# First stage of a two-layer GLA / NSA decoder step: ScalarE's first copy, ScalarE's order, products of zeros ahead of the turning

## What is computed

```python
def rms_norm(x, g):
    y = x * lax.rsqrt(jnp.mean(x * x, axis=-1, keepdims=True) + EPS)
    return y * g
...
hp = rms_norm(xp, norm_mix[i])
hs = rms_norm(xs, norm_mix[i])
...
z = h @ w_in
q, k, v, r, gr = jnp.split(z, ...)
log_alpha = jax.nn.log_sigmoid(gr @ w_gate2 + b_gate) / GLA_TAU
```

## Time and profile before

| | us |
|---|---|
| median of 3 runs | 1865.19 |
| lowest and highest run | 1858.73, 1870.34 |
| the profiled execution | 1865.75 |
| its span, first to last instruction | 1863.9 |
| PE busy in the span | 1728.0 |
| VectorE, ScalarE, GpSimd busy | 985.2, 724.1, 445.4 |

### The profile page before, as it was taken

How to read it: one execution, slowest core, us unless ns; L and a number is a source line. 1 busy time by engine, 2 the same in 40 slices (tenths; PEclk the granted TensorE clock), 3 DMA queues, 4 the chain that set the end, 5 groups by cost and what they waited for, 6 DMA issues and landing times.

```text
span 1863.9 us, 33488 instructions
## 1 busy us (share of the span) xinstructions
PE 1728.0 (93%) x13943; PEld 1602.3 (86%) x13951; DVE 985.2 (53%) x1518; ACT 724.1 (39%) x1227; POOL 445.4 (24%) x378
## 2 busy tenths in 40 slices
PE   7999989999999998999898897898889999999996
PEld 6989767999999997999787796676757999999996
DVE  5070457644444455466777865778524644444443
ACT  4352343332323232332455644677652332323230
POOL 4354234000000002444222122687803000000000
PEclk9999879999999999999899898899998999999998
DMA  4212123222222222331322110002373322222211
GB/s 173 91 46 91 49 97 111 118 91 91 91 90 90 90 90 98 109 119 46 114 103 84 53 58 1 1 2 91 136 316 137 136 91 91 91 90 90 90 45 46
DMA packets 25617, 170.13 MB, mean 91 GB/s; under 512 B 2146, under 2 KB 13970, under 8 KB 15706
## 3 DMA queue, kind: packets, MB, share of 16 engines
q1 hardware_dynamic: 22346, 131.18, 18.8%
q0 software_dynamic: 3152, 37.26, 5.3%
HBM read 156.26 MB, written 12.17 MB: 90 GB/s over the span
## 4 chain that ended last, share of the span: by engine, by line
PE 75%; DVE 12%; ACT 7%; issue 3%; POOL 2%; DMA 1%; ACTq 0%; SPq 0%; DVEq 0%; PEldq 0%; POOLq 0%
PE slot L2241 55%; PE slot L2497 3%; PE slot L2210 2%; ACT phase L1486 2%; PE slot L2505 2%; PE slot L2324 2%; POOL phase L1003 1%; PE slot L2475 1%; DVE xt_rest L1967 1%; PE slot L2285 1%; PE slot L2635 1%; PE slot L2695 1%; DVE base L1581 1%; DVE phase L1682 1%; PE slot L2579 1%
## 5 line engine op out<-in xcount | busy, mean ns | idle before, releaser
L1285 ACT ACTIVATE w_high<-weights 128x1024 fp32r<-128x1024 f32 x128 | 135.3, 1060 | 258.4 <-PE slot L2241 250.0
L2241 PE MATMUL slot<-h_high,w_high 128*128 128x260 f32 x1024 | 208.0, 284 | 0.0
L2241 PE MATMUL slot<-h_high,w_rest 128*128 128x260 f32 x1024 | 207.5, 284 | 0.0
L2241 PE MATMUL slot<-h_rest,w_high 128*128 128x260 f32 x1024 | 207.4, 284 | 0.0
L2241 PE MATMUL slot<-u_high,w_high 128*128 128x260 f32 x1024 | 206.3, 283 | 0.0
L2241 PE MATMUL slot<-u_rest,w_high 128*128 128x260 f32 x1024 | 206.0, 283 | 0.0
L2241 PE MATMUL slot<-u_high,w_rest 128*128 128x260 f32 x1024 | 206.0, 283 | 0.0
L1818 DVE TENSOR_TENSOR w_rest<-weights,w_high 128x1024 fp32r<-128x1024 f32 x128 | 156.0, 1222 | 31.5 <-ACT w_high L1285 31.5
L2241 PEld LDWEIGHTS slot<-h_high,w_high 128*128 128x128 f32 x1024 | 159.2, 190 | 0.2
L2241 PEld LDWEIGHTS slot<-h_high,w_rest 128*128 128x128 f32 x1024 | 159.0, 190 | 0.0
L2241 PEld LDWEIGHTS slot<-h_rest,w_high 128*128 128x128 f32 x1024 | 158.8, 190 | 0.0
(11 more groups left out here) (419 smaller groups left out, 4132.5 us busy)
## 6 DMA issues: line engine op xcount, KB each, us to landing
weights<-in_wt SPq DMA_DIRECT2D x47, 2048.0 KB, 7.8
weights<-in_state SPq DMA_DIRECT2D x2, 2048.0 KB, 8.8
out<-weights SPq DMA_DIRECT2D x2, 2048.0 KB, 8.3
weights<-in_w SPq DMA_DIRECT2D x2, 2048.0 KB, 9.0
out<-phase SPq DMA_DIRECT2D x6, 512.0 KB
x_rows<-residual SPq DMA_DIRECT2D x1, 2080.0 KB, 6.8
residual<-x_rows SPq DMA_DIRECT2D x1, 2080.0 KB, 11.0
phase<-in_x_prompt SPq DMA_DIRECT2D x2, 1024.0 KB, 6.5
```

The source lines that it names most:

```text
L1285: nc.scalar.activation(w_part[k % 4][0][:, :, :], ring[:, s, :, 128 * (k % 4):128 * (k % 4) + 128], ACT.Copy).then_inc(w_high_ready, 1)
L2241: last = mm(ps[0:w.shape[2], a, 0:HT], w[:, k, :], m[:, k, HT * a:HT * a + HT], start=k == 0 and w is high and m is x_high, stop=k == DC - ...
```

## The change

Four things change, all in the first stage.

- ScalarE begins with a copy of one column (`eps_col` to a column of `rstd_col`, which is written anew later). It waits only for `bf_ready`, and the table load goes with it.
- The high part of `wgr` is made after chunk 2 and no longer after chunk 4. It takes the place of a square, so the squares follow one chunk later from there on.
- The high part of the first weight piece is made after the square that follows chunk 6, ahead of chunk 7, and no longer behind chunk 7 and the square of chunk 6. The squares of the last three chunks then come in a row.
- PE makes nine products of zeros ahead of the first turning, into slot 0. They wait for `bf_ready`. The function that makes them is moved up in the code.

```diff
             act.wait_ge(bf_ready, 5)
+            link(nc.scalar.activation(rstd_col[:, 0:1], eps_col, ACT.Copy))
             act.wait_ge(ident_in, 48)
             for c in range(DC):
                 act.wait_ge(x_ready, c + 1)
                 nc.scalar.activation(gh_part[0][:, c, :], xT[:, c, :], ACT.Copy, scale=P("norm")[:, c:c + 1])\
                     .then_inc(mixed_high_ready, 1)
-                if c:
-                    square_of_input(c - 1)
-                if c == 4:
+                if c == 2:
                     act.wait_ge(gla_small_in, 48)
                     nc.scalar.activation(wgr_part[0][:, :, :], wgr, ACT.Copy).then_inc(wgr_high_ready, 1)
-            gla_weights_high(0)
+                elif c:
+                    square_of_input(c - 1 - (c > 2))
+                if c == 6:
+                    gla_weights_high(0)
+            square_of_input(DC - 2)
             square_of_input(DC - 1)
             for n in range(1, 4):
                 gla_weights_high(n)
...
+            def zero_products(ps, n):
+
+                for _ in range(n):
+                    mm(ps[:, 0, :], identb, zerosb, start=True, stop=True, skip_group_check=True)
+
...
+            pe.wait_ge(bf_ready, 5)
+            ps, _ = claim(pe, ("xt", 0))
+            zero_products(ps, 9)
             pe.wait_ge(ident_in, 48)
```

More of the change, by code:

```diff
@@ L2227, in _ @@
                     .then_inc(fu, 1)
-            def zero_products(ps, n):
-                for _ in range(n):
-                    mm(ps[:, 0, :], identb, zerosb, start=True, stop=True, skip_group_check=True)
             def split_products(ps, weights, x, wait=None):
```

## The result

The changed kernel takes 1872.9 us (median of 20 runs, 1867.08 to 1879.89) where the kernel before, measured again beside it, takes 1869.19 (median of 20, the three of the table among them, 1858.48 to 1870.34). The ratio is 1.0031, 95% interval 1.0021 to 1.0042: **3.9 to 7.8 us slower**, about 5.8. That is within 1%, but 1864.2 was forecast and 1869.3 was the end of the range; the change lost time instead of winning 1 us. The ratio is estimated from all the runs and is not the quotient of the two medians, which lie 3.7 us apart. The median of before is 4 us higher than that of the three runs of the table; that explains part of the distance to 1864.2, but not the loss.

A forecast was written before the change was run, and what follows sets the result against it. The prediction took PE as the bound, with only the first stage to win. An earlier start, less the zeros' time and the low clock, gave 0.28 to 1.66 us, middle 1.0: 1864.2 us, range 1857.7 to 1869.3.

The forecast's parts named there:

- What bounds the kernel: Whole kernel: PE, busy 1728.0 of 1863.9 us; only its standstills or half-speed time ahead of about 36 us can be won.
- Table load: ScalarE's start: the load moves behind a one-column copy taken as free; VectorE's first rest can start 0.76 us sooner.
- Products of zeros, their time: Ahead of PE's first turning: nine take 3.9 us, 0.2 lost; first rest 0.56 to 1.66 us sooner, depending on clock level.
- Order on ScalarE: First stage: moved weight copies cost the same; the sums' slack before the mean of squares shrinks from 0.40 to 0.23 us.
- a rival: Level staying high to the rank product, 0.13: GpSimd's 0.75 us pause between weight rests adds up to 2.2 us.
- The level behind it: Rank product: begins at the low clock again; depending on when that stretch ends, the gain is 0.28 to 1.66 us.
- The sum: Whole kernel: 0.28 to 1.66 us won, middle 1.0, forecast 1864.2 us; nothing behind 36 us gives it back.
- Level stays high: Clock stays high up to the rank product: 1.9 to 3.8 us won, middle 2.9, 1862.3 us; chance 0.13.
- zeros eat the gain: Ahead of the turnings: products of zeros start 0.56 us later against the input, gain gone, 1865.2 us; chance 0.14.
- ScalarE stalls: First stage: ScalarE waits for the first weight tile, 2.9 us slower, 1868.1 us; chance 0.04.
- The range: Whole kernel: 1857.7 to 1869.3 us, from the scatter of three runs of one kernel moved by 1.0.

The follow-up runs named there:

- run 3: ScalarE's part of the change alone, without the products of zeros ahead of the turnings, against the kernel before: 1868.11 us, ratio 0.9994.
- run 9: The whole change with four products of zeros ahead of the turnings instead of nine, against the kernel before: 1868.08 us, ratio 1.0004.
- run 5: The nine products of zeros alone, ScalarE as before, plus 62 met waits behind the first stage, against the kernel before: 1870.34 us, ratio 1.0032.
- run 8: The kernel before with 72 met-wait instructions ahead of the first turning and nothing else, against the kernel before: 1871.60 us, ratio 1.0024.
- run 7: The kernel before with only 62 met waits spread behind the first stage, as a control, against the kernel before: 1869.93 us, ratio 1.0024.
- run 11: The whole change with 13 instead of 22 products of zeros ahead of layer 1's first product, against the kernel before: 1866.81 us, ratio 0.9996.
- run 4: The whole change with 11 instead of 20 products of zeros ahead of layer 0's output projection, against the kernel before: 1871.85 us, ratio 1.0013.
- run 1: The kernel before with only 18 met-wait instructions added on PE ahead of the first turning, against the kernel before: 1874.64 us, ratio 1.0028.
- run 2: The whole change with 110 met-wait instructions on PE ahead of the rank product, against the kernel before: 1869.78 us, ratio 1.0011.

## Why the prediction was wrong, point by point

**What bounds the kernel: right.** PE still has no gap ahead of the mean of squares.

**Table load: right.** It waits for nothing, starts at 0.75 and is over at 2.03. The copy costs 0.20, in ScalarE's idle time. ScalarE's part alone brought the rank product 0.5 us forward (run 3), where the step has 0.76; the first turning of that run started at 7.82, 0.4 us later than before.

**Products of zeros, their time: right, at the better end.** Nine took 4.02 us (3.9 predicted); the turnings behind them shortened to 0.27, so the first rest came at 10.16 (9.95 for that end) and chunk 7's copy 1.61 sooner (1.66). That takes all nine and ScalarE's part together: with four the turnings stay at 0.42 (run 9), and without ScalarE's part the rank product starts at 20.98 (run 5), no sooner than before.

**Order on ScalarE: right in the part that decides, wrong in one size.** The first weight piece went at 18.79 without a stall and the part of chunk 7 at 19.73. But the slack of the sums was to shrink from 0.40 to 0.23 and grew to 33.19 - 31.24 = 1.95 us. Before, the two large sums took 7.43 us:

```profile
23.51 7.43 DVE L1626 TENSOR_TENSOR phase<-phase 128x2080 f32<-128x2080 f32 x2 [1.22 <-ACT phase L1079]
```

After, they take 5.66, and the difference is in the first one, 2.31 us long and 4.09 before. It starts at 22.77, in a pause of GpSimd from 22.29 to 23.05; before, it started at 23.51 beside a weight rest that had begun at 23.03. Why it is then so much shorter isn't shown. I had that pause only in a rival, priced by a copy of 0.69 and an addition of 2.71, which are two operations; it came without the rival's condition and gave 7.43 - 5.66 = 1.77. Since PE is the bound, it changed nothing.

**The level behind it: right in kind, its size in part by luck.** Table of stretches of after:

```profile
core 0: us, PE busy (x) PEld busy (x) DVE busy (x) ACT busy (x) POOL busy (x), PEclk, DMA share, GB/s
7.90:18.10 10.20, 5.77 (x40) 4.11 (x38) 8.61 (x13) 7.15 (x12) 0.45 (x1) 0.99 1.03 398
18.10:25.00 6.90, 5.73 (x28) 3.86 (x29) 6.29 (x5) 6.88 (x11) 4.34 (x2) 0.52 0.77 324
25.00:36.00 11.00, 11.00 (x91) 10.38 (x90) 7.11 (x4) 2.71 (x3) 8.50 (x3) 1.00 0.00 0
```

The granted clock is at its upper level (2.4 GHz) while the turnings run, near its lower one (1.2 GHz) from 18.1 to 25.0 us, and the rank product's first pairs are 0.64 long. The 96 products to the mean of squares took 14.08 us (13.45 before), so of 1.61 only 0.97 was left. The step had two ends: a low stretch that keeps its length, or one that ends at the same moment as before. In the records of the clock the upper level is there from 24.8 us after and from 25.0 before, so it was nearly the second, while the start was at its better end; that the two together gave the middle, 1.0, is luck. This size varies: without the change's first stage the 96 took 12.94 to 13.87 (runs 8 and 7), with it 12.97 to 14.12 (runs 11 and 4). The Trainium skill, "TensorE: Matmul & The Clock Gate", Part 4, says that transposes don't engage the full clock; here 32 of them ran at 0.27 behind nine plain products, as 32 others do at the program's end. They can raise the level too, and here the runs decide against the page: in run 1, where nothing but turnings had run on PE, they went from 0.42 to 0.27 us at 15.0 (rows in the last section).

**The sum: this failed.** The step is "Everything behind 36 us follows PE, so nothing gives it back". The products of zeros were priced by their run time, 0.2 us, and by what they do to the level. They are also 18 instructions in PE's program, and PE's program has a loop 1650 us later whose instructions are kept from round to round or fetched anew, depending on where it begins. That term was missing: -1.0 + 5.6 = **+4.6**, and 3.9 to 7.8 was measured. Run 1 gives the term without the stage (+5.2), run 11 the stage without the term (-0.7 by its ratio, not clear of zero).

**The rivals.** "Level stays high" fell with the 0.64 pairs; "zeros eat the gain" and "ScalarE stalls" with the rows above. The slower side had a rival of the wrong kind. The trace of before held the clue: 87 packets of instructions of which none falls in 186 us of the second MLP, while PE passes the loop's products twice. That is a loop that is kept, and an edit which moves it was to be asked what happens when it isn't.

**The range** was set by the scatter of runs, 11.6 us. The miss is no scatter: it is there in the ratio.

## What to carry to other kernels

An instruction added anywhere ahead of a loop moves the loop, so compare the instruction packets and the "issue" standstills at the loop's jumps before and after, and put the loop back by dropping as many instructions elsewhere; time that as well, since run 4 did it at another place than run 11 and gained nothing. A gain of 1 us at the start of such a kernel is smaller than this effect, and than the scatter of whole runs; show it in the stage's own rows, and read the granted clock beside each run's time. Waits used as padding are no neutral control: measure them alone.

## What the runs showed of the hardware that was not expected

- A loop of 1578 PE instructions is fetched once, or again for every round: nine packets of 16 KB at each jump, with two standstills, 1.8 to 2.2 and 0.9 to 1.7 us. Of the places tried, 137 and 147 of 256 do it to the second MLP's loop; the first MLP's loop did not stall at any place it had, 144 among them. What rule decides it stays open.
- An instruction of waits that are already met costs PE 0.10 to 0.11 us where PE has nothing else to do: 110 of them from 14.4 to 25.75 us (run 2), and 72 from about 3.5 to 11.51 (run 8).
- Nine products of zeros of 512 columns, ending as the first turning starts, bring the 32 turnings from 0.42 to 0.27 us each; four, after which PE is idle for 1.93 us, don't. Nor are products needed: in run 1, without any, the turnings themselves ran at 0.42 from 7.60 and at 0.27 from 15.01, and the record of the clock stands at 1.00 from 14.9 to 18.3 us. In before and in run 8 they stayed at 0.42 to the end. The rows of run 1:

```profile
13.81 1.11 PE L2227 MATMUL slot<-base,phase 128*128 128x128 f32 x4
...
15.01 0.66 PE L2227 MATMUL slot<-base,phase 128*128 128x128 f32 x4
```

- While the turnings of run 9 took 0.42, the clock column stood at 1.00, as in the earlier trace rows; its table of stretches:

```profile
4.00:17.50 13.50, 11.57 (x44) 7.42 (x42) 7.28 (x11) 5.94 (x10) 0.45 (x1) 1.00 1.03 392
```

That 1.00 is no measurement: the first record of the clock in that trace begins at 26.0 us, in the trace of before at 25.0. So at a program's start durations have to be read beside that column.
